# Paged forgetting-attention on one core: preparation two row tiles ahead, prompt part read in place, sample part interleaved

## The chip, the cores and the metric

The kernel runs on one core of one Trainium2 chip. The metric is the device time of one execution in microseconds (us), a median over runs. One execution is one step of a small hybrid decoder (prompt of 1,024 rows, and 8 sample sequences of 8 rows each); the change touches the attention part of its first layer only.

## The reference, cut to what matters

The attention has 8 heads of 64 columns. q and k are normed per head (an RMS norm with a gain), and a log-forget value per row and head, summed along the sequence, is added to the scores.

```python
def fox_attend_prompt(q, k, v, logf):
    Fk = jnp.cumsum(logf, axis=1)
...
    s = einsum('bqhd,bkhd->bhqk', qi, k) * Dh ** -0.5
    s = s + Fq[..., :, None] - Fk[..., None, :]
    s = jnp.where(kpos[None, :] <= qpos[:, None], s, -jnp.inf)
    p = jax.nn.softmax(s, axis=-1)
    return einsum('bhqk,bkhd->bqhd', p, v)

def fox_attend_sample(q, k, v, logf, pool_k, pool_v, pool_lf, page_table):
    k_past = pool_k[page_table]
    v_past = pool_v[page_table]
    lf_past = pool_lf[page_table]
    k_all, v_all = concat(k_past, k), concat(v_past, v)
    Fk = jnp.cumsum(concat(lf_past, logf), axis=1)
...
```

The sample's scores, decay, mask, softmax and values follow as for the prompt; a sequence has 8 pages of 128 past rows. Everything is in 32-bit floats. The output also holds k, v and the log-forgets of the new rows (`fk`, `fv`, `flf`).

## The kernel before, in words

Five engines run their own instruction streams: TensorE (PE, with weight loads shown as PEld), VectorE (DVE), ScalarE (ACT), GpSimd (POOL) and SyncE (SP, which issues most DMAs). The kernel is written with explicit semaphores; each function below is one block, and all engines meet at the end of a block. In the attention three blocks follow one another; what stands on an engine inside one is its program order.

`fox_prep` (L1166) walks over N = 9 row tiles: 8 prompt tiles of 128 rows and one tile of the 64 sample rows. First the log-forgets are made (`fl`, `nab`, `l1`, `lf`), and PE sums them into `psF` by 36 small matmuls (L1281, L1282). Then for each tile: ACT squares the 1,024 columns of q and k (L1265); DVE sums them per head and takes the mean (L1326, L1327) and copies two columns of forget sums into the rows (L1331, L1332); POOL takes the power -1/2 (L1231); DVE scales the rows (L1334); POOL multiplies the gains in (L1235, twice 128x512); PE transposes 16 heads into the one buffer `ps` (L1291); ACT and DVE copy half of it each to `qkA`, two extra rows of which carry the forget sums (L1254, L1318); ACT issues the DMA of `fk` (L1258). ACT closes the block with the sigmoid of the gate `sog` (L1270).

`fox_prompt` (L1341) loads v by one DMA (L1368), which lands in `spare`, the place of the residual `trunk_xT`. In 4 turns of a hardware loop (two heads each) DVE copies q, k and v of a head to staging buffers (L1471 to L1473); then for 16 units PE makes scores and adds the causal mask by a matmul (L1394, L1397), DVE takes the maximum (L1478), ACT the exponential (L1442), PE transposes the probabilities (L1419), ACT copies them (L1453), and PE multiplies with the values (L1406). At a turn's end the outputs are transposed (L1428) and copied (L1456).

`fox_sample` (L1509) handles the 8 sequences one after the other in a hardware loop. SP reads the page table and for each of the 8 pages of a sequence reads one page number and issues three DMAs, log-forgets `lp`, keys `kp` and values `vp` (L1573, L1575, L1577), two sequences ahead of use. The residual saved in `x_kept` (4,352 KB) is brought back by a DMA that ACT issues at the block's start (L1652). Per sequence: DVE spreads the log-forgets (L1695), PE transposes them (L1609), DVE scans them into `F` (L1701); PE turns the keys page by page (L1618), ACT copies them (L1660), PE makes scores of 128 columns (L1623); DVE adds decay and mask into `st` (L1708 to L1710) and takes the maximum (L1711); ACT exponentiates (L1662); PE transposes the probabilities (L1633, L1635), ACT copies them (L1664), PE multiplies with 8 pages of values and the new rows (L1640, L1641); DVE masks the heads (L1715), PE transposes (L1645), DVE sums (L1718). PE holds `pe.wait_ge(reduced, i + 1)` at the end of each sequence, so nothing of the next one starts before.

Of the kernel before, what the change touches and what calls it, by code (L numbers as in the profile page):

```python
# [1165 lines left out]
def fox_prep(nc, C, p, q_gain, k_gain, b_f, qkA, sog, qTs, kTs, lfs, fk, fv, flf):  # L1166
# [6 lines left out]
    N = NT + 1  # L1173
    with Phase(nc, "fxp") as ph:
        pf = ph.sb("pf", [P, 2, 2 * FOX_W])
        gains = ph.sb("gains", [P, 2, DH])
        bf = ph.sb("bf", [P, H])
        sq = ph.sb("sq", [P, 2, 2 * H * DH])
        ss, ms, rstd = (ph.sb(n, [P, 2 * H]) for n in ("ss", "ms", "rstd"))
        fl, nab, l1, lf = (ph.sb(n, [P, N, H]) for n in ("fl", "nab", "l1", "lf"))  # L1180
        qa = ph.sb("qa", [P, 2, 2 * H, A])
        qs = ph.sb("qs", [P, 2 * H, DH])
        ps = ph.ps("ps", [P, 4, 4, P])
        psF = ph.ps("psF", [P, 512])
        F = ph.sb("F", [P, 2, NT, H])
        pf_in = [ph.sem(f"pf_in{b}") for b in range(2)]
        outs = [ph.sem(f"outs{b}") for b in range(2)]
        (params_in, fv_out, sog_in, fl_in, zeroed, nabbed, logged, lf_done, lf_out, summed, squared, meaned,
         rooted, scaled, gained, turned, stored_a, stored_d, dve_step, act_step) = (ph.sem(s) for s in (
             "params_in", "fv_out", "sog_in", "fl_in", "zeroed", "nabbed", "logged", "lf_done", "lf_out", "summed",  # L1190
             "squared", "meaned", "rooted", "scaled", "gained", "turned", "stored_a", "stored_d",
             "dve_step", "act_step"))
# [9 lines left out]
        @block.sync  # L1202
        def _(sp):
            sp.dma_start(gains[:, 0, :], q_gain.partition_broadcast(P)).then_inc(params_in, 16)
            sp.dma_start(gains[:, 1, :], k_gain.partition_broadcast(P)).then_inc(params_in, 16)
            for i in range(N):
                r = rows_of(i)
                if i >= 2:
                    sp.wait_ge(scaled, i - 1)
                sp.dma_start(pf[:r, i % 2, :], p[i * P:i * P + r, 0:2 * FOX_W]).then_inc(pf_in[i % 2], 16)  # L1210
                if i == 1:
                    sp.dma_start(fv, p[:, 2 * FOX_W:3 * FOX_W]).then_inc(fv_out, 16)
                    sp.dma_start(sog[:, 0:NT, :], p[0:SEQ, 3 * FOX_W:4 * FOX_W].rearrange("(n p) c -> p n c", p=P))\
                        .then_inc(sog_in, 16)
                    sp.dma_start(sog[:NS, NT, :], p[SEQ:, 3 * FOX_W:4 * FOX_W]).then_inc(sog_in, 16)
            sp.wait_ge(lf_done, 1)
            sp.dma_start(flf[0:SEQ].rearrange("(n p) c -> p n c", p=P), lf[:, 0:NT, :]).then_inc(lf_out, 16)
            sp.dma_start(flf[SEQ:], lf[:NS, NT, :]).then_inc(lf_out, 16)
            sp.wait_ge(fv_out, 16)
            sp.wait_ge(lf_out, 32)  # L1220

        @block.gpsimd
        def _(pool):
            pool.memset(fl[:], 0.0).then_inc(zeroed, 1)
            pool.wait_ge(params_in, 32)
            pool.tensor_scalar(gains[:, 0, :], gains[:, 0, :], DH ** -0.5, None, ALU.mult).then_inc(params_in, 1)
            pool.wait_ge(params_in, 33)
            for i in range(N):
                r = rows_of(i)
                pool.wait_ge(meaned, i + 1)  # L1230
                pool.tensor_tensor(rstd[:r], ms[:r], C["half"][:r, :2 * H], ALU.pow).then_inc(rooted, 1)  # L1231
                pool.wait_ge(scaled, i + 1)
                for n in range(2):
                    t = rows_out(i)[:, n * H:(n + 1) * H, 0:DH]
                    ins = pool.tensor_tensor(t, t, bc(gains[:r, n, :], 1, H), ALU.mult)  # L1235
                ins.then_inc(gained, 1)

        @block.scalar
        def _(act):
# [5 lines left out]

            act.wait_ge(nabbed, 1)
# [3 lines left out]

            def finish(i):
                act.wait_ge(turned, i + 1)
                if i < NT:
                    ins = act.copy(qkA[:A, 0:8, i * P:(i + 1) * P], ps[:A, 0:2].rearrange("p a b t -> p (a b) t"))  # L1254
                else:
                    ins = act.copy(qTs[:], ps[:, 0, :, :NS])
                ins.then_inc(stored_a, 1)
                act.dma_start(fk[i * P:i * P + rows_of(i), :].rearrange("t (h d) -> t h d", d=DH),  # L1258
                              rows_out(i)[:, H:, 0:DH]).then_inc(outs[i % 2], 16)
            for i in range(N):  # L1260
                r = rows_of(i)
                act.wait_ge(pf_in[i % 2], 16 * (i // 2 + 1))
                if i >= 2:
                    act.wait_ge(meaned, i - 1)
# [6 lines left out]
            act.activation(sog[:NS, NT, :], sog[:NS, NT, :], ACT.Sigmoid)  # L1271
            act.wait_ge(outs[0], 16 * ((N + 1) // 2))
            act.wait_ge(outs[1], 16 * (N // 2))

        @block.tensor
        def _(pe):
            pe.wait_ge(lf_done, 1)
            for i in range(NT):
                o = psF[:, i * H:(i + 1) * H]
                for j in range(i):  # L1280
                    pe.matmul(o, C["ones"][:], lf[:, j, :], start=(j == 0), stop=False)  # L1281
                mm = pe.matmul(o, C["tri"][:], lf[:, i, :], start=(i == 0), stop=True)  # L1282
            mm.then_inc(summed, 1)
            for i in range(N):
                pe.wait_ge(gained, i + 1)
                if i:
                    pe.wait_ge(stored_a, i)
                    pe.wait_ge(stored_d, i)
                if i < NT:
                    for n in range(2 * H):  # L1290
                        mm = pe.transpose(ps[:A, n // 4, n % 4, :], qa[:, i % 2, n, :], C["ident"][:])  # L1291
                else:
                    for n in range(H):
                        mm = pe.transpose(ps[:, n // 4, n % 4, :NS],
                                          qs[:NS, 2 * n:2 * n + 2, :].rearrange("p a d -> p (a d)"),
                                          C["ident"][:NS, :NS])
                mm.then_inc(turned, 1)

        @block.vector
        def _(dve):  # L1300
            step = Chain(dve, dve_step)
            step(dve.memset(qa[:], 1.0))
            dve.wait_ge(fl_in, 48)
            step(dve.tensor_tensor(fl[:], fl[:], bc(bf[:], 1, N), ALU.add))
            dve.scalar_tensor_tensor(nab[:], fl[:], -1.0, fl[:], ALU.mult, ALU.min).then_inc(nabbed, 1)
            dve.wait_ge(logged, 1)
            dve.scalar_tensor_tensor(lf[:], fl[:], 0.0, l1[:], ALU.min, ALU.subtract).then_inc(lf_done, 1)
            dve.wait_ge(lf_done, 1)
            dve.tensor_copy(lfs[:], lf[:NS, NT, :])
# [2834 lines left out]
```

## Time and profile before

| | us |
|---|---|
| median of 3 runs | 4562.07 (4560.52 to 4562.45) |
| the profiled execution's own time | 4567.51 |
| its span, first to last instruction | 4565.8 |
| attention: preparation, prompt, sample | from 971 to 1658 of the span |

### The profile page before, as it was taken

The numbers are of one execution on the slowest core, as the hardware profiler recorded it, in microseconds if no ns is written. First come the engines' busy times: TensorE is split into PE (matmuls) and PEld (weight loads), VectorE is DVE, ScalarE is ACT, GpSimd is POOL, SyncE is SP. The second block draws the span as 40 slices with busy tenths as digits, with TensorE's granted clock in tenths as the row PEclk, the third lists the DMA queues.
The fourth block names the chain that finished last, engine by engine and source line by source line (L and its number), as shares of the span: only waits on it lengthen the run. The fifth ranks groups of instructions, "written<-read, shape, count | busy, mean of one in ns | idle before, by whom it ended". The sixth has DMA issues, their size and how long they took to land. (4 is left out here: it accounts for less than half of the span.)

```text
span 4565.8 us, 65914 instructions
## 1 busy us (share of the span) xinstructions
PE 3912.7 (86%) x24414; PEld 3665.5 (80%) x24414; DVE 2287.5 (50%) x4117; ACT 935.8 (20%) x1738; POOL 1240.7 (27%) x946
## 2 busy tenths in 40 slices
PE   8997688666977778999999789794887779999996
PEld 8996577655754467999999789794787779999996
DVE  3265677433322223655556476414773346655554
ACT  2000332123331111211111122202452021111112
POOL 3222233222000012423323133223443233323321
PEclk9998788756678888999999999996887889999997
DMA  4254111121024311111111022223222221111111
GB/s 171 88 157 156 57 43 25 25 79 49 0 78 129 120 39 40 56 37 51 36 51 46 11 72 90 75 68 79 71 52 66 74 46 51 46 37 51 36 41 48
DMA packets 372258, 290.39 MB, mean 64 GB/s; under 512 B 108647, under 2 KB 333991, under 8 KB 371729
## 3 DMA queue, kind: packets, MB, share of 16 engines
q1 hardware_dynamic: 315656, 228.95, 17.1%
q10 hardware_dynamic: 56460, 59.56, 3.9%
q8 instruction: 87, 1.43, 0.1%
q14 instruction: 55, 0.45, 0.0%
HBM read 216.43 MB, written 73.99 MB: 64 GB/s over the span
## 5 line engine op out<-in xcount | busy, mean ns | idle before, releaser
L983 PE MATMUL fup_acc<-ffn_high,fup_wh 128*128 128x364 f32 (+1 forms) x2112 | 699.5, 331 | 48.6 <-POOL fup_wl L907 26.9
L984 PE MATMUL fup_acc<-ffn_low,fup_wh 128*128 128x364 f32 (+1 forms) x2112 | 698.3, 331 | 0.0
L985 PE MATMUL fup_acc<-ffn_high,fup_wl 128*128 128x364 f32 (+1 forms) x2112 | 696.1, 330 | 0.0
L983 PEld LDWEIGHTS fup_acc<-ffn_high,fup_wh 128*128 128x128 f32 x2112 | 400.4, 190 | 50.6 <-POOL fup_wl L907 25.6
L1143 DVE TENSOR_TENSOR trunk_xT<-fup_dn,trunk_xT 128x364 f32<-128x364 f32 x528 | 282.7, 535 | 245.6 <-PE fup_dn L1001 245.6
L984 PEld LDWEIGHTS fup_acc<-ffn_low,fup_wh 128*128 128x128 f32 x2112 | 400.5, 190 | 0.0
L985 PEld LDWEIGHTS fup_acc<-ffn_high,fup_wl 128*128 128x128 f32 x2112 | 400.3, 190 | 0.0
L999 PE MATMUL fup_dn<-fup_gh,fup_dh 128*128 128x364 f32 (+1 forms) x1056 | 348.4, 330 | 21.3 <-issue 21.3
L1000 PE MATMUL fup_dn<-fup_gl,fup_dh 128*128 128x364 f32 (+1 forms) x1056 | 347.3, 329 | 0.0
L1001 PE MATMUL fup_dn<-fup_gh,fup_dl 128*128 128x364 f32 (+1 forms) x1056 | 346.7, 328 | 0.0
L335 PE MATMUL p_acc<-p_wh,even_in_high 128*128 128x296 f32 (+1 forms) x936 | 281.4, 301 | 10.6 <-DVE even_in_low L374 7.9
L336 PE MATMUL p_acc<-p_wl,even_in_high 128*128 128x296 f32 (+1 forms) x936 | 281.8, 301 | 0.0
L337 PE MATMUL p_acc<-p_wh,even_in_low 128*128 128x296 f32 (+1 forms) x936 | 280.6, 300 | 0.0
L1056 ACT ACTIVATE fup_conv<-fup_hp,fup_cur 128x1024 f32<-128x1024 f32 x88 | 109.6, 1246 | 574.4 <-DVE fup_hs L1118 574.4
L1131 DVE SCALAR_TENSOR_TENSOR fup_conv<-fup_hp,fup_cur,fup_conv 128x1024 f32<-128x1024 f32 x176 | 225.4, 1280 | 3.1
L999 PEld LDWEIGHTS fup_dn<-fup_gh,fup_dh 128*128 128x128 f32 x1056 | 199.3, 189 | 21.8 <-issue 21.8
L907 POOL TENSOR_TENSOR fup_wl<-fup_ws,fup_wh 128x1024 fp32r<-128x1024 f32 x88 | 211.1, 2399 | 7.0
L983 PE MATMUL gqkv_acc<-odd_in_high,gqkv_wh 128*128 128x364 f32 (+1 forms) x576 | 191.4, 332 | 24.2 <-DVE odd_in_low L1086 21.8
L924 POOL COPY fup_cur<-ffn_taps 128x4 f32 (+1 forms) x88 | 16.4, 187 | 711.0 <-DVE fup_conv L1132 711.0
L1115 DVE TENSOR_TENSOR fup_hp<-fup_acc,fup_rs 128x364 f32<-128x364 f32 (+1 forms) x264 | 125.4, 506 | 159.7 <-PE fup_acc L985 145.9
L1000 PEld LDWEIGHTS fup_dn<-fup_gl,fup_dh 128*128 128x128 f32 x1056 | 200.0, 189 | 0.0
L1001 PEld LDWEIGHTS fup_dn<-fup_gh,fup_dl 128*128 128x128 f32 x1056 | 199.1, 189 | 0.0
(719 smaller groups left out, 8674.2 us busy)
## 6 DMA issues: line engine op xcount, KB each, us to landing
fup_ws<-in_ffn_w_up SPq DMA_DIRECT2D x88, 512.0 KB, 4.0
fup_ds<-in_ffn_w_down SPq DMA_DIRECT2D x22, 1024.0 KB, 5.9
fs_kp<-in_cache_fox_k SPq DMA_DIRECT2D x64, 256.0 KB, 2.7
fs_vp<-in_cache_fox_v SPq DMA_DIRECT2D x64, 256.0 KB
ev<-p_o ACTq DMA_DIRECT2D x104, 148.0 KB, 1.8
p_ws<-in_ev_w_in SPq DMA_DIRECT2D x12, 1184.0 KB, 7.1
qkv<-gqkv_conv ACTq DMA_DIRECT2D x24, 544.0 KB
gqkv_ws<-in_od_w_in SPq DMA_DIRECT2D x24, 512.0 KB, 4.1
```

Source lines behind the costliest of these rows:

```text
L335: pe.matmul(ps, xh[:, k, cols], wh[:, b, k], start=(k == 0), stop=False)
L336: pe.matmul(ps, xh[:, k, cols], wl[:, b, k], start=False, stop=False)
L337: mm = pe.matmul(ps, xl[:, k, cols], wh[:, b, k], start=False, stop=(k == KD - 1))
L907: pool.tensor_tensor(wl[:, b], ws[:, b], wh[:, b], ALU.subtract).then_inc(low, 1)
L983: pe.matmul(ps, wh[:, b, k], xh[:, k, c0:c0 + w_], start=(k == 0), stop=False)
L984: pe.matmul(ps, wh[:, b, k], xl[:, k, c0:c0 + w_], start=False, stop=False)
L985: mm = pe.matmul(ps, wl[:, b, k], xh[:, k, c0:c0 + w_], start=False, stop=(k == KD - 1))
L999: pe.matmul(ps, dh[:, s, cols], gh[:, s, c0:c0 + w_], start=(s == 0), stop=False)
L1000: pe.matmul(ps, dh[:, s, cols], gl[:, s, c0:c0 + w_], start=False, stop=False)
L1001: mm = pe.matmul(ps, dl[:, s, cols], gh[:, s, c0:c0 + w_], start=False, stop=(s == 1))
L1131: dve.scalar_tensor_tensor(cp, hp[:, b, j:j + SEQ], cur[:, b, j:j + 1], cp, ALU.mult, ALU.add)
L1143: dve.tensor_tensor(xT[:, t, c0:c0 + w_], dn[m % 2][:, :w_], xT[:, t, c0:c0 + w_], ALU.add).then_inc(added, 1)
```

## The change

Preparation: the tile buffer `pf` has 4 places, and squares and means are issued two tiles ahead of the scaling (AHEAD = 2); `ps` has two buffers; the gains are applied by ACT while it copies both halves from `ps` (a scale per partition, `gcol`), and for `fk` by one DVE multiply (`ko`), which SP stores; the forget sums take 7 adds on DVE (`before`) and two matmuls; SP loads v into `spare` in this block already. Prompt: q, k and v are read where they are, the turns are written out instead of looped, and SP gathers the page table and the 64 pieces of log-forgets of the sample part. Sample: all log-forgets are transposed and scanned once, ahead of the sequences; scores are made 512 columns at a time; decay and mask are added on PE by matmuls (`spread` with `F`, the identity with `causal`); maximum and exponential read PSUM; PE works on the next sequence's keys and scores between one sequence's probabilities, values and `collect`; SP reads a page number for each DMA; the return of `x_kept` is issued by ACT at sequence 1.

```diff
@@ fox_prep, scalar: order of squares and stores
-            for i in range(N):
...
-                act.activation(sq[:r, i % 2], pf[:r, i % 2], ACT.Square).then_inc(squared, 1)
-                if i:
-                    finish(i - 1)
-            finish(NT)
-            act.wait_ge(sog_in, 32)
-            act.activation(sog[:, 0:NT, :], sog[:, 0:NT, :], ACT.Sigmoid)
+            for i in range(AHEAD, N + AHEAD):
+                if i < N:
+                    square(i)
+                if i == N - 1:
+                    act.wait_ge(sog_in, 32)
+                    act.activation(sog[:, 0:NT, :], sog[:, 0:NT, :], ACT.Sigmoid)
+                    act.activation(sog[:NS, NT, :], sog[:NS, NT, :], ACT.Sigmoid)
+                store(i - AHEAD)
@@ fox_prep, vector: one tile
+                if i + AHEAD < N:
+                    mean(i + AHEAD)
...
+                dve.wait_ge(rooted, i + 1)
+                step(dve.tensor_tensor(rows_out(i)[:, :, 0:DH], pf[:r, i % RING, :].rearrange("p (h d) -> p h d", d=DH),
+                                       bc(rstd[:r, i, :], 2, DH), ALU.mult))
+                dve.sem_inc(scaled, 1)
...
+                dve.tensor_tensor(ko[:r, b], rows_out(i)[:, H:, 0:DH], bc(gains[:r], 1, H), ALU.mult).then_inc(ko_done, 1)
@@ fox_sample, sync
+            def load(dst, pool, n, sem):
+                page = sp.value_load(table[0:1, n:n + 1], min_val=0, max_val=N_POOL - 1)
+                sp.dma_start(dst, pool[bass.ds(page, 1)].rearrange("o p c -> p (o c)")).then_inc(sem, 16)
+            for i in seqs:
+                if i >= 2:
+                    sp.wait_ge(k_turned, NU * (i - 1))
+                for g in range(NPG):
+                    load(kp[:, i % 2, g, :], pool_k, i * NPG + g, k_in[i % 2][g // HALF])
+                if i >= 2:
+                    sp.wait_ge(valued, i - 1)
+                for g in range(NPG):
+                    load(vp[:, i % 2, g, :], pool_v, i * NPG + g, v_in[i % 2])
@@ fox_sample, tensor: a key turn and a score of 512 columns
+                for g in range(HALF):
+                    mm = pe.transpose(PS[:, 5 + n % RING, g * P:(g + 1) * P],
+                                      kp[:, i % 2, c * HALF + g, m * P:(m + 1) * P], ident[:])
...
+                pe.matmul(S[:, c * 512:(c + 1) * 512], qx[:, i, m, :], kT[:, n % RING, :], start=(m == 0), stop=False)\
+                    .then_inc(k_used, 1)
```

The order on ACT in the preparation, from the two first squares on (`fxp_sq` is the squares' buffer, `fxp_ps` the turned heads). Before, the store of a tile and its DMA stand ahead of one square:

```order
L1265 ACTIVATE fxp_sq<-fxp_pf 128x1024 x2
L1254 COPY fox_p_qkA<-fxp_ps 66x8x128
L1258 DMA out_fk<-fxp_qa 1024x1x64
L1265 ACTIVATE fxp_sq<-fxp_pf 128x1024
L1254 COPY fox_p_qkA<-fxp_ps 66x8x128
```

And now:

```order
L1266 ACTIVATE fxp_sq<-fxp_pf 128x1024 x2
L1288 ACTIVATE fxp_nab<-fxp_nab 128x72
L1290 ACT_TABLE_LOAD
L1290 ACTIVATE fxp_l<-fxp_nab 128x72
L1266 ACTIVATE fxp_sq<-fxp_pf 128x1024
L1276 ACTIVATE fox_p_qkA<-fxp_ps,fxp_gcol 66x8x128 x2
L1266 ACTIVATE fxp_sq<-fxp_pf 128x1024
L1276 ACTIVATE fox_p_qkA<-fxp_ps,fxp_gcol 66x8x128 x2
```

Three squares (tiles 0, 1 and 2) now stand ahead of the first store, two before; from there on squares and stores still alternate.

The order on DVE in the preparation of the changed kernel, from the first tile of the loop on (`ss` and `ms` are sum and mean, `qa` the scaled rows):

```order
L1327 TENSOR_REDUCE fxp_ss<-fxp_sq 128x16
L1328 TENSOR_SCALAR fxp_ms<-fxp_ss 128x16
L1359 COPY fxp_qa<-fxp_F 128x8
L1360 COPY fxp_qa<-fxp_F 128x8
L1362 TENSOR_TENSOR fxp_qa<-fxp_pf,fxp_rstd 128x16x64
L1367 TENSOR_TENSOR fxp_ko<-fxp_qa,fxp_gains 128x512
```

The first two rows are the sum and mean of tile i + 2, the others belong to tile i; before, all were of one tile.

The order on PE in the sample part of the changed kernel, one stage (L1599 turns keys, L1609 scores, L1628 probabilities, L1638 values, L1645 collects, L1616 to L1620 decay and mask):

```order
L1599 MATMUL fs_PS<-trunk_ident,fs_kp 128x128 x12
L1628 MATMUL fs_PS<-trunk_ident,fs_pr 128x64 x8
L1629 MATMUL fs_PS<-trunk_ident,fs_pr 8x64
L1609 MATMUL fs_PS<-fs_kT,fs_qx 64x512
L1599 MATMUL fs_PS<-trunk_ident,fs_kp 128x128 x4
...
L1638 MATMUL fs_PS<-fs_vp,fs_pT 64x512 x8
L1639 MATMUL fs_PS<-fs_vn,fs_pT 64x512
...
L1645 MATMUL fs_PS<-fs_onehot,fs_om 128x8 x4
L1609 MATMUL fs_PS<-fs_kT,fs_qx 64x512 x3
L1616 MATMUL fs_PS<-fs_F,fs_spread 64x512 x2
```

Twelve key turns of sequence i + 1 stand between the exponential that PE waits for and the probabilities of sequence i; before, nothing of another sequence stood there (L1628 of `fs_N`, then L1633).

## Rows read from the trace of the kernel before

**Rows 1.** Windows: length, busy PE, PEld, DVE, ACT, POOL (instructions), granted clock, DMA share, GB/s.
```profile
971.00:999.20 28.20, 15.53 (x72) 15.44 (x72) 2.72 (x6) 3.70 (x5) 0.56 (x2) 0.50 0.60 203
999.20:1064.10 64.90, 30.10 (x136) 22.47 (x136) 35.05 (x53) 14.76 (x15) 47.07 (x27) 0.50 0.33 86
1080.60:1343.40 262.80, 244.90 (x1216) 196.48 (x1216) 82.12 (x213) 96.22 (x203) 0.00 (x0) 0.73 0.00 0
1343.40:1367.80 24.40, 0.66 (x4) 0.50 (x4) 2.99 (x16) 0.37 (x1) 4.58 (x5) 0.50 0.96 354
1367.80:1657.90 290.10, 225.86 (x1160) 138.59 (x1160) 61.25 (x117) 52.79 (x96) 0.00 (x0) 0.82 0.32 103
1139.80:1180.70 40.90, 39.18 (x134) 30.60 (x134) 11.99 (x29) 13.16 (x29) 0.00 (x0) 0.50 0.00 0
```
**Rows 2.** Timeline, start of the preparation: start, duration, instruction, [idle before].
```profile
983.30 0.23 DVE L1307 SCALAR_TENSOR_TENSOR fxp_lf<-fxp_fl,fxp_l 128x72 f32<-128x72 f32 x1 [1.90 <-ACT fxp_l L1249]
...
999.16 0.22 DVE L1311 COPY fxp_F<-fxp_psF 128x64 f32<-128x64 f32 x1 [15.43 <-PE fxp_psF L1282]
...
1004.08 1.23 DVE L1334 TENSOR_TENSOR fxp_qa<-fxp_pf,fxp_rstd 128x1024 f32<-128x1024 f32 x1 [2.96 <-POOL fxp_rstd L1231]
```
**Rows 3.** Timeline, the steps of one row tile in the preparation.
```profile
1007.75 3.62 PE L1291 MATMUL fxp_ps<-trunk_ident,fxp_qa 128*66 128x128 f32 x16 [8.63 <-POOL fxp_qa L1235]
...
1011.41 1.01 ACT L1254 COPY fox_p_qkA<-fxp_ps 66x1024 f32<-66x1024 f32 x1 [26.25 <-PE fxp_ps L1291]
...
1012.32 1.06 ACT L1265 ACTIVATE fxp_sq<-fxp_pf 128x1024 f32<-128x1024 f32 x1
1013.41 1.22 DVE L1326 TENSOR_REDUCE fxp_ss<-fxp_sq 128x16 f32<-128x1024 f32 x1 [0.46 <-ACT fxp_sq L1265]
...
1014.66 0.17 DVE L1327 TENSOR_SCALAR fxp_ms<-fxp_ss 128x16 f32<-128x16 f32 x1
```
**Rows 4.** Timeline, the scaling of the last tile and the end of the preparation.
```profile
1059.16 1.22 DVE L1334 TENSOR_TENSOR fxp_qs<-fxp_pf,fxp_rstd 64x1024 f32<-64x1024 f32 x1 [3.00 <-POOL fxp_rstd L1231]
...
1065.98 3.62 ACT L1270 ACTIVATE fox_sog<-fox_sog 128x4096 f32<-128x4096 f32 x1
```
**Rows 5.** Timeline, start of the prompt block, and of its second turn.
```profile
1070.36 0.38 SPq L1368 DMA_DIRECT2D trunk_xT<-out_fv  x1
...
1080.61 0.79 PE L1394 MATMUL fx_S<-trunk_xT 66*128 66x128 f32 x2 [16.51 <-DVE fx_vh L1473]
...
1144.19 1.28 ACT L1442 ACT_TABLE_LOAD   x1
1144.35 0.29 DVE L1478 TENSOR_REDUCE fx_mx<-fx_S 128x1 f32<-128x128 f32 x1 [1.97 <-PE fx_S L1397]
```
**Rows 6.** Groups by line, sample part: busy, mean ns, idle before them and releaser.
```profile
L1609 PE MATMUL fs_L<-trunk_ident,fs_lx 128*64 128x128 f32 x64 | 15.0, 416 | 36.5 <-DVE fs_qx L1699 36.5
...
L1633 PE MATMUL fs_psK<-trunk_ident,fs_pr 64*128 64x64 f32 x64 | 8.1, 298 | 34.6 <-ACT fs_pr L1662 34.6
```
**Rows 7.** Timeline, single steps of the first sequence of the sample part.
```profile
1368.70 0.38 SPq L1577 DMA_DIRECT2D fs_vp<-in_cache_fox_v  x1
...
1369.94 0.33 SPq L1573 DMA_DIRECT2D fs_lp<-in_cache_fox_logf  x1
...
1372.91 0.42 PEld L1618 LDWEIGHTS fs_psK<-trunk_ident,fs_kp 128*128 128x128 f32 x4 [0.17 <-issue]
...
1385.57 1.22 DVE L1711 TENSOR_REDUCE fs_mx<-fs_st 64x1 f32<-64x1032 f32 x1
1386.83 1.15 ACT L1662 ACTIVATE fs_pr<-fs_st,fs_mx 64x1032 f32<-64x1032 f32 x1 [4.54 <-DVE fs_mx L1711]
...
1391.56 0.23 PEld L1640 LDWEIGHTS fs_O<-fs_vp,fs_pT 128*64 128x64 f32 x1 [0.62 <-issue]
...
1396.23 0.14 PEld L1640 LDWEIGHTS fs_O<-fs_vp,fs_pT 128*64 128x64 f32 x1 [0.29 <-issue]
```
**Rows 8.** The page's list of DMA issues: count, size of one, us to landing.
```profile
fs_kp<-in_cache_fox_k SPq DMA_DIRECT2D x64, 256.0 KB, 2.7
```

More of the change, by code:

```diff
@@ L1224, in _ @@
             pool.memset(fl[:], 0.0).then_inc(zeroed, 1)
[L1225 to L1227 removed]
+            pool.memset(before[:, 0, :], 0.0).then_inc(zeroed, 1)
+            pool.memset(qa[:], 1.0).then_inc(qa_set, 1)
             for i in range(N):
@@ L1230, in _ @@
                 pool.wait_ge(meaned, i + 1)
[L1231 to L1236, printed above, removed]
+                pool.tensor_tensor(rstd[:r, i, :], ms[:r, i, :], C["half"][:r, :2 * H], ALU.pow).then_inc(rooted, 1)
         @block.scalar
@@ L1276, in _ @@
         def _(pe):
[L1277 to L1283, printed above, removed]
-            for i in range(N):
[L1285 to L1295, printed above, removed]
+            pe.wait_ge(lf_done, 2)
@@ new lines, in _ @@
+            pe.matmul(psF, C["tri"][:], lf[:, 0:NT, :].rearrange("p n h -> p (n h)"), start=True, stop=False)
+            pe.matmul(psF, C["ones"][:], before.rearrange("p n h -> p (n h)"), start=False, stop=True).then_inc(summed, 1)
+            for i in range(N):
+                pe.wait_ge(scaled, i + 1)
+                if i == 1:
+                    pe.wait_ge(F_done, 1)
+                if i >= 2:
+                    pe.wait_ge(stored, i - 1)
+                for n in range(2 * H):
+                    if i < NT:
+                        mm = pe.transpose(ps[i % 2][:A, n // 4, n % 4, :], qa[:, i % 2, n, :], C["ident"][:])
+                    else:
+                        h, k = n % H, n // H
+                        mm = pe.transpose(ps[i % 2][:DH, 2 * k + h % 2, h // 2, :NS], qs[:NS, n, :],
@@ L1430, in body @@
                     mm.then_inc(o_turned, 1)
-            with pe.Fori(0, turns) as i:
+            for i in range(turns):
                 body(i)
@@ L1455, in body @@
                     act.wait_ge(o_turned, i * 2 + (half + 3))
-                    act.copy(mixT[:, bass.ds(i, 1), half * 512:(half + 1) * 512].rearrange("p o t -> p (o t)"),
+                    act.copy(mixT[:, i, half * 512:(half + 1) * 512],
                              psM.rearrange("p a b -> p (a b)")).then_inc(mixed, 1)
             act.sem_inc(copied, 1)
-            with act.Fori(0, turns) as i:
+            for i in range(turns):
                 body(i)
@@ new lines, in _ @@
+            for u in range(8):
+                score(0, u)
+                if u < 5:
+                    turn_keys(0, u + 3)
+            pe.wait_ge(spread_done, 1)
+            pe.wait_ge(masks_done, 1)
+            pe.wait_ge(scanned, 2)
+            pe.wait_ge(gate_copied, 1)
+            decay(0)
+            for i in seqs:
+                nxt = i + 1 < NB
+                if nxt:
+                    for u in range(3):
+                        turn_keys(i + 1, u)
+                turn_probs(i)
+                if nxt:
+                    for u in range(2):
+                        score(i + 1, u)
+                        turn_keys(i + 1, u + 3)
+                values(i)
+                if nxt:
+                    for u in range(2, 5):
+                        score(i + 1, u)
+                        turn_keys(i + 1, u + 3)
+                collect(i)
+                if nxt:
+                    for u in range(5, 8):
+                        score(i + 1, u)
+                    decay(i + 1)
```

507 lines of the change are left out of this document (253 added, 254 removed).

## The prediction, made before the changed kernel ran

> **What bounds the kernel now.** I read the windows first, cut at the blocks of the attention [rows 1]. The preparation (971 to 1070) has no full engine: in its tile loop of 64.9 us PE is busy 30.1, DVE 35.1, ACT 14.8, POOL 47.1, at a granted clock of 0.50. So a chain binds it, not a load. The prompt part is bound by PE: 244.9 of 262.8 us, at a mean clock of 0.73. The sample part begins with 24.4 us of loading (PE busy 0.66, DMA engines 0.96 busy at 354 GB/s), and in the 290.1 us behind it PE is busy 225.9 at a clock of 0.82 while DMA is 0.32 busy. Then I read the groups by line for the sample part, for PE's idle time: 34.6 us stand before the probabilities, released by the exponential, and 36.5 before the transposes of log-forgets, released by DVE's setup of the next sequence [rows 6]. Both are 4.3 to 4.6 us in each of 8 sequences; the reader is to see that a sequence's softmax and its neighbour's setup lie bare on PE, and that in them PE has nothing else to do. The timeline gives the durations of single steps.
>
> The sum is made against the profiled execution (4567.5 us; 5.4 over the median of the runs shown); I take 5.4 off at the end. A measurement of this kernel can tell about 0.2% (9 us) from no change.
>
> **Preparation, the start.** The 36 small matmuls are removed: PE spends 15.5 us on 72 passes [rows 1], and DVE waits 15.43 for them [rows 2]. In their place stand 7 dependent DVE adds and two matmuls. An add costs about the 0.23 us of the neighbouring small operation, so 1.6, and I give the matmuls 0.6. The log-forgets are done at 983.5 [rows 2], so the forget sums are copied by 986.5 rather than 999.5. Behind them DVE does the mean of tile 2 (1.4), the column copies (0.3) and the scaling (1.23): the first tile is scaled at about 990.5 against 1005.3 [rows 2], 15 us earlier.
>
> **Preparation, the loop.** "Two tiles ahead" suggests that squares run free. The order says otherwise. On ACT the square of tile i+2 stands behind the stores of tile i-1, and on DVE the mean of tile i+2 stands ahead of the scaling of tile i. So the scaling of tile i waits for: transposes of i-1, its two stores, square of i+2, mean of i+2, scaling of i. By rows: transposes 3.62 (at the half clock, which the loop has now), two ACT copies 1.01 each with 0.91 from one start to the next, together 1.9, square 1.06 [rows 3], reduce and mean 1.42 from start to end [rows 3], column copies 0.2, scaling 1.23 [rows 2], and some 0.2 of handing over: 9.7 us. Now a tile takes (1059.16 - 1004.08) / 8 = 6.9 [rows 2, 4]. The gains on POOL and one DVE copy are off the path, but a whole chain of three engines is closed in a ring. Six such steps lead from the scaling of tile 0 to that of tile 6: 990.5 + 58 = 1048.7. From there no square is left: tiles 6, 7 and 8 take PE 3.7, 3.7 and about 2.3, and the last stores 1.5; the sigmoid with its table load (1.28 as in the prompt's row, and some 4.2 for both parts [rows 4, 5]) now lies under these transposes. The block ends near 1060 instead of 1070. **Saves 10.** Bounds: if PE's clock rose, transposes take half, a tile 7.9, and it saves 20; if the loads, which now bring v as well before the loop, delay the first tile by 6 us, 4.
>
> By the Trainium skill (TensorE: Matmul & The Clock Gate, section on the array's architectural detail) the queues of ScalarE and VectorE are strictly first in, first out, and only PE may pull weight loads ahead. This trace agrees: the square at 1012.32 follows the copy of 1011.41 at once and did not pass it [rows 3]. If a square could pass a waiting store, tiles would run at PE's pace, which is the second rival below.
>
> **Prompt.** v is loaded in the block before, so the first score comes about 1.1 us after the block's start rather than 1080.61 - 1070.36 = 10.25 [rows 5]: 9.1 saved. The staging copies at a turn's start lie under PE's output transposes and cost nothing now; what cover they had is not needed further. In three turns the table load (1144.19 for 1.28) holds the exponential back by 0.83 behind the maximum, which is done at 1144.64 [rows 5]; with written-out turns I take it as gone, 2.5. The 64 gathers on SP lie beside 262.8 us in which DMA moves nothing [rows 1]. **Saves 11.5**; bounds 8 (the table load stays, the gathers slow one start) to 20 (the half-clock stretch at a turn gets shorter).
>
> **Sample, one stage.** PE's work on a sequence at full clock, from rows: 32 key turns at 0.106 each (0.42 for 4) 3.4 [rows 7]; passes of 512 columns at 0.43 (0.14 and 0.29 [rows 7]): 16 for scores, 4 for decay, 18 for values, 16.3; some 29 small ones at under 0.106, about 2.4. Together 22.1. Idle: maximum 1.22 and exponential 1.15 plus 0.4 of accumulator and handing over, less 1.3 of key turns that now stand there [rows 7], 1.5; and 1.0 for collect and values waiting on copies. A stage is 24.6, and a sequence is 36.3 now (290.1 / 8).
>
> **Sample, loads.** SP reads a page number for each load now. From the issue of vp to the next lp 1.24 us pass, which is one read and one issue [rows 7]. So 17 loads a stage take 20.5, below 24.6 but not far. At the start, the first values wait for the key turns of sequence 1, hence for 21 loads: 21 x 1.24 + 2.7 of landing [rows 8] is 28.7, and with 5 for key turns, probabilities and their copy the values of sequence 0 begin at 33.7.
>
> **Sample, sum.** 33.7 + 6 x 24.6 + 22 (the last stage turns no keys ahead) + 7.7 values + 2.4 tail = 213 at full clock, against 24.4 + 290.1 = 314.5. The clock is the open term. Before the values PE stands idle for 4.3 us, and the values then begin at 0.85 a pass and end at 0.43 [rows 6, 7]; the mean is 0.82. The new bare waits are 1.5 at most, so I expect it higher. If the clock were full, nothing is added; if the mean stayed 0.82, 36% of a stage would lie at half, which makes 24.6 into 30.0, 38 over seven stages. I take a third, 13, nearer the full end since two thirds of the idle time is gone. So 226, **saves 88.5** (63 to 101). The return of `x_kept` (4,352 KB) now falls among page loads: at 354 GB/s [rows 1] it is 12.6 us of DMA, from 0 (hidden by the loads' lead of about a stage) to 12.6. I take 0, as page loads occupy a third of the DMA time now.
>
> By the Trainium skill (DMA: Bandwidth & Descriptors, Issuing engines are not separate DMA queues), DMAs of SP and ACT interleave on the same 16 engines, which speaks against a free return; by it the sample part would be 239. The trace's 0.96 DMA share at the sample's start [rows 1], when both load, agrees.
>
> Together 10 + 11.5 + 88.5 = 110: 4457.5 for a profiled execution, **4452** as a median.
>
> **Rivals.** (a) *The clock stays at half through the whole sample part.* The prompt part shows that PE may be busy 39.18 of 40.90 us with a clock of 0.50 throughout [rows 1], so being busy alone does not bring it up; against it, the sample part has 0.82 with more gaps. A stage then has 44.2 of PE's work and 2 idle, 46.2, and the sample part 379: 64.5 more than before, 4562 - 21.5 + 64.5 = **4605**. It decides from a stage of 42 us on (336 less 44 for start and end, over 7), that is with 80% of the stage at half clock. (b) *The preparation really runs two ahead*: a tile is PE's 3.7, the block ends at about 1028, 32 more saved: **4420**. The order speaks against it. (c) *SP binds the sample part*: if each load cost the whole 2.2 of today's set of three, a stage is 17 x 2.2 = 37 and nothing is saved there: about **4545**. Three issues in a set with one read speak against it. (d) *Full clock in every stage*: **4439**. (e) *Clock as low as now, 0.82*: 25 more, **4477**.
>
> **Numbers.** Forecast with its neighbourhood (4443 to 4468) 0.59; (a) 0.05; (b) 0.06; (c) 0.05; (d) 0.12; (e), with the return of `x_kept` exposed, 0.13. The range reaches from (b) past (e) with the return: 4418 to 4490; it leaves out (a) and (c), one in ten. Faster by over 0.2%: all but (a) and the 0.02 between the signs, 0.93; the same 0.02; slower 0.05.
>
> **What would show it.** The start: the copy of forget sums at about 986. The loop: 9.7 us from one scaling to the next, each square right behind a store, and DVE idle before the mean, released by ACT's square; wrong if 3.7 or 6.9. The prompt: first score a microsecond after the block begins, no table load at a turn. The sample: stages of 25 to 28 us, idle before the probabilities near 1.5 each, key loads never the releaser but at the start, a clock over 0.9. What would make the prediction wrong above all is the clock in the sample part, then the start of its loads.

## The result, and the profile after

The changed kernel takes 4436.33 us (median of 4 runs, 4427.01 to 4457.23) against 4562.26 before: a ratio of 0.973, with a 95% interval of 0.969 to 0.976. That is 126 us faster; 4452 was predicted. The profiled executions differ by 4567.51 - 4435.05 = 132.5 us. Every median below is taken over the fast runs, which leaves out one run of e10 that took 11393 us.

I cut both traces at the same four instructions: the memset of `fl` on POOL (preparation), that of the mask (prompt), the copy of the turned gate `sgT` on ACT (sample), and the first cast of the output projection behind them (end).

| block, us | before | after | won | predicted |
|---|---|---|---|---|
| preparation | 97.7 | 83.7 | 14.0 | 10 |
| prompt | 274.0 | 243.1 | 30.9 | 11.5 |
| sample | 313.4 | 231.1 | 82.3 | 88.5 |
| outside the attention | | | 5.3 | 0 |

The windows of the changed kernel (columns as in [rows 1]), first its blocks, then five stretches of the prompt part:

```profile
969.50:985.50 16.00, 1.12 (x4) 0.93 (x4) 6.78 (x24) 4.87 (x6) 7.76 (x5) 0.50 0.81 289
985.50:1053.60 68.10, 28.04 (x144) 21.70 (x144) 25.82 (x46) 29.63 (x29) 27.66 (x7) 0.62 0.39 128
1054.70:1297.10 242.40, 225.53 (x1220) 182.10 (x1220) 71.14 (x192) 92.69 (x201) 0.50 (x1) 0.80 0.02 2
1297.10:1321.00 23.90, 18.30 (x74) 9.04 (x74) 7.07 (x16) 5.05 (x9) 4.17 (x5) 0.79 0.72 220
1321.00:1528.20 207.20, 188.51 (x728) 76.95 (x728) 17.35 (x25) 45.68 (x89) 0.00 (x0) 0.97 0.50 160
1092.60:1119.20 26.60, 24.09 (x167) 20.07 (x166) 9.24 (x26) 10.53 (x22) 0.00 (x0) 1.00 0.07 5
1119.80:1146.80 27.00, 26.32 (x88) 20.24 (x87) 6.32 (x16) 8.64 (x22) 0.00 (x0) 0.50 0.02 2
1147.20:1180.80 33.60, 30.60 (x213) 25.47 (x211) 11.18 (x31) 14.00 (x29) 0.00 (x0) 1.00 0.00 1
1181.40:1208.00 26.60, 25.92 (x86) 19.82 (x86) 6.32 (x16) 7.63 (x20) 0.00 (x0) 0.50 0.00 0
1208.60:1294.00 85.40, 77.25 (x524) 63.49 (x523) 29.25 (x80) 38.12 (x82) 0.00 (x0) 1.00 0.00 1
```

The reader is to see two things. PE worked during the first loading of the sample part (18.3 of 23.9 us, where it had 0.66 of 24.4 [rows 1]). And the prompt part still is PE's, but at a clock of 0.80 instead of 0.73. Both begin with a stretch at half (35 us before, 38 after). Behind the ends of the first two turns the clock now lay at half for 27 us each, where one such stretch before was 40.9 [rows 1], and from 1208.6 to 1294.0, across the third turn's end, it stayed at full.

One tile of the preparation, in the timeline of the changed kernel (start, duration, instruction, [idle before]):

```profile
994.80 1.22 DVE L1362 TENSOR_TENSOR fxp_qa<-fxp_pf,fxp_rstd 128x1024 f32<-128x1024 f32 x1
...
996.13 3.62 PE L1313 MATMUL fxp_ps<-trunk_ident,fxp_qa 128*66 128x128 f32 x16 [5.94 <-DVEq L1364]
...
999.79 2.11 ACT L1276 ACTIVATE fox_p_qkA<-fxp_ps,fxp_gcol 66x1024 f32<-66x1024 f32 x2 [6.51 <-PE fxp_ps L1313]
1001.80 1.05 ACT L1266 ACTIVATE fxp_sq<-fxp_pf 128x1024 f32<-128x1024 f32 x1
1002.88 1.22 DVE L1327 TENSOR_REDUCE fxp_ss<-fxp_sq 128x16 f32<-128x1024 f32 x1 [6.02 <-ACT fxp_sq L1266]
...
1004.36 1.22 DVE L1362 TENSOR_TENSOR fxp_qa<-fxp_pf,fxp_rstd 128x1024 f32<-128x1024 f32 x1
```

This is the ring of the prediction: it goes from DVE to PE, to ACT and back to DVE, each starts when the one above it ends, and from one scaling to the next it is 9.56 us (9.7 worked out, 6.9 before [rows 2, 4]). Each of the three engines is idle for about 6 of them.

### The profile page after: what moved, and what is told of

Same layout as the page of the kernel before. It is cut to its first block and busy times, and to the rows that moved or that the text cites. A ratio compares the mean times of both kernels' runs of the same rounds, so it can differ in the third digit from the quotient of the medians.

```text
span 4433.3 us, 64635 instructions
## 1 busy us (share of the span) xinstructions
PE 3850.3 (87%) x23996; PEld 3574.0 (81%) x23996; DVE 2240.9 (51%) x4008; ACT 939.4 (21%) x1746; POOL 1227.3 (28%) x929
## 5 line engine op out<-in xcount | busy, mean ns | idle before, releaser
L999 PEld LDWEIGHTS fup_dn<-fup_gh,fup_dh 128*128 128x128 f32 x1056 | 199.3, 189 | 21.8 <-issue 21.8
L983 PE MATMUL gqkv_acc<-odd_in_high,gqkv_wh 128*128 128x364 f32 (+1 forms) x576 | 191.3, 332 | 27.5 <-DVE odd_in_low L1086 25.0
```

The costliest lines, as they stand in the source:

```text
L983: pe.matmul(ps, wh[:, b, k], xh[:, k, c0:c0 + w_], start=(k == 0), stop=False)
L999: pe.matmul(ps, dh[:, s, cols], gh[:, s, c0:c0 + w_], start=(s == 0), stop=False)
```

## The experiments

Each kernel was timed beside the kernel before, and the ratio is to that. Blocks and "clock", the granted clock of the prompt block, are those of one profiled execution each.

| kernel | preparation | prompt (clock) | sample | median | ratio to before |
|---|---|---|---|---|---|
| before | 97.7 | 274.0 (0.73) | 313.4 | 4562.26 | |
| changed | 83.7 | 243.1 (0.80) | 231.1 | 4436.33 | 0.973 (0.969 to 0.976) |
| e1 preparation alone | 84.2 | 269.5 (0.76) | 310.3 | 4547.05 | 0.996 (0.995 to 0.997) |
| e2 prompt alone | 97.7 | 252.4 (0.80) | 310.2 | 4536.39 | 0.994 (0.992 to 0.997) |
| e3 sample alone | 97.6 | 278.3 (0.72) | 233.3 | 4488.88 | 0.984 (0.981 to 0.986) |
| e4 mean behind | 57.9 | 230.1 (0.86) | 235.2 | 4405.41 | 0.967 (0.964 to 0.969) |
| e5 turns written out | 97.8 | 232.3 (0.88) | 310.1 | 4535.18 | 0.994 (0.992 to 0.996) |
| e6 paired units | 57.7 | 252.6 (0.78) | 235.9 | 4444.09 | 0.975 (0.971 to 0.979) |
| e7 return at start | 60.6 | 230.1 (0.86) | 244.0 | 4414.04 | 0.967 (0.963 to 0.971) |
| e8 pairs grouped | 57.2 | 230.2 (0.86) | 233.7 | 4407.43 | 0.966 (0.963 to 0.970) |
| e9 turns joined | 57.3 | 213.7 (0.91) | 231.1 | 4396.27 | 0.962 (0.958 to 0.965) |
| e10 stall at turns | 57.6 | 267.3 (0.74) | 235.6 | 4445.67 | 0.972 (0.970 to 0.974) |
| e11 changed again | 89.9 | 223.3 (0.88) | 237.3 | 4434.14 (one run) | |
| e12 turns joined, again | 57.9 | 213.7 (0.91) | 231.7 | 4392.89 | 0.963 (0.962 to 0.965) |

### One part alone: e1, e2, e3

e1 puts the changed `fox_prep`, without its load of v, into the kernel before; e2 the changed `fox_prompt`, with v loaded at its start and without the gathers; e3 the changed `fox_sample`, with the gathers on SP in the old prompt block:

```diff
 e2, fox_prompt, sync
-            for n in range(NB * NPG):
-                page = sp.value_load(table[0:1, n:n + 1], min_val=0, max_val=N_POOL - 1)
...
+            sp.dma_start(v[:], fv[0:SEQ, :].rearrange("(t p) c -> p t c", p=P)).then_inc(v_in, 16)
```

> The changed preparation (without its early load of v) in the kernel before; prompt and sample as before. Theory: the new order closes a ring of 9.6 us a tile, so only the 15 us at the start and the hidden sigmoid are won against 6.9 us a tile: the block is 14 us shorter (98.1 to about 84), the whole 0.3% faster (4548). Rival: some of the 14 us comes with the early load or with the clock of the neighbouring blocks; then the block is shorter by less than 10.

> The changed prompt part (read in place, turns written out) in the kernel before; v is still loaded at the block's start, nothing is gathered. Theory: the 30.5 us that the block lost are 9.1 of waiting for v and some 21 of clock, and the clock is won by the written-out turns, which leave fewer gaps at a turn's start: this kernel's block is 18 to 24 us shorter than 273. Rival A: the clock has nothing to do with the code, only with when the block starts, so the shares of half clock may come out as before or anywhere: 0 to 24. Rival B: only the table loads go: 2.5 shorter, half-clock stretches as before.

> The changed sample part in the kernel before, with the gathers of log-forgets and of the page table on SP in the old prompt block. Theory: parts add up, the sample block takes 232 us instead of 314.6 with stages of 27 us; the whole 82 us faster (4480). Rival: the sample part gains from the clock with which the new prompt block hands over (full at its end there, half in the kernel before): then the start is slower and the block takes 240 or more.

The preparation block is 13.5 us shorter, the prompt block 21.6, the sample block 80.1. The parts add up within the intervals: by the ratios 18.7 + 26 + 73.5, with 9.1 for the early v, 127 of 124 to 126. The sample part doesn't need the new prompt block ahead of it. e2 shows that 21.6 us of the prompt part have nothing to do with the wait for v.

Of the sample part's gain the windows show what kind of time went. PE's idle time in the block fell from 88 us (314.5, less 0.66 and 225.86 busy [rows 1]) to 24 (231.1, less 18.30 and 188.51), and its busy time from 227 to 207. So about three quarters are idle time that is now filled. How much each edit gives (the early scan, scores of 512 columns, decay on PE, the next sequence's keys in the gaps) no run takes apart.

### The ring of the preparation: e4

```diff
             for i in range(N):
                 r, b = rows_of(i), i % 2
-                if i + AHEAD < N:
-                    mean(i + AHEAD)
...
                 dve.tensor_tensor(ko[:r, b], rows_out(i)[:, H:, 0:DH], bc(gains[:r], 1, H), ALU.mult).then_inc(ko_done, 1)
+                if i + AHEAD < N:
+                    mean(i + AHEAD)
```

> The changed kernel with one thing moved in the preparation: DVE does the mean of tile i + 2 behind the scaling of tile i, not ahead of it. Theory of the ring: the scaling no longer waits for the square that stands behind the last tile's store; a round of the chain now spans three tiles, (9.6 + 3 of POOL) / 3 = 4.2 us a tile, near PE's 3.7; the block is some 30 us shorter (84 to about 54), the whole near 4405. Rival: the tile time is set by something else (the loads of pf, the stores, PE at half clock), and the tiles stay above 8 us: 4430.

The block falls from 83.7 to 57.9 us, and the median by 31. Two rows of its timeline show what became of the wait:

```profile
1008.30 1.22 DVE L1327 TENSOR_REDUCE fxp_ss<-fxp_sq 128x16 f32<-128x1024 f32 x1 [1.87 <-ACT fxp_sq L1266]
...
1013.80 1.23 DVE L1360 TENSOR_TENSOR fxp_qa<-fxp_pf,fxp_rstd 128x1024 f32<-128x1024 f32 x1 [0.48 <-POOL fxp_rstd L1251]
```

DVE waited about 6 us for each square of the ring (6.02 above); now it waits 1.87 here, 2.57 at one other tile, and not at all at the rest, and a scaling waits at most 0.79 for POOL's power. The scalings of tiles 0 and 7 start 34.5 us apart, 4.9 a tile; 4.2 was expected. The ring is shown: nothing but the place of one pair of instructions differs. (Of the median's 31 us the preparation explains 26; the profiles' prompt blocks differ as well, for which see e11.)

### What the prompt part gained: e5, e6

e5 keeps the staging copies and the wait for v, and only writes the turns out, on PE, ACT and DVE:

```diff
-            with pe.Fori(0, turns) as i:
+            for i in range(turns):
                 body(i)
```

> The kernel before with its prompt part's four turns written out instead of looped; the staging copies and the wait for v stay. It tells apart what the prompt part owes to the written-out turns and to reading in place. Theory A: the loop's costs at a turn (table load, branch) let the clock fall longer: the block drops from 274 to about 254, as with the whole changed prompt part. Theory B: it is the staging, which holds the scores of a head until three copies are through: the block stays at 268 or more. Rival: neither, only where in time the block lies; then its share of half clock differs from both with no relation to the edit.

The block takes 232.3 us, 41.7 less than before, where 254 was expected, at a clock of 0.88. The profile is of the fastest of 8 runs; by the medians e5 is 31.5 us faster than the kernel before, and e2 29. Either way the written-out turns alone are enough for the prompt part's gain beyond the wait for v, and nothing has to be put down to reading in place. In the three profiles with the loop (before, e1, e3) the block took 269.5 to 278.3 us, and written out, with the wait for v of 9.1, 232.3 and 252.4 (e5, e2). The windows of e5: the block, the stretch at half behind the first turn, and the one after it:

```profile
1071.50:1302.80 231.30, 202.11 (x1220) 165.01 (x1220) 83.22 (x216) 92.45 (x202) 0.87 (x1) 0.88 0.03 11
1139.60:1145.60 6.00, 4.88 (x20) 4.11 (x20) 2.33 (x6) 1.63 (x4) 0.00 (x0) 0.50 0.01 3
1146.60:1237.60 91.00, 83.12 (x551) 67.45 (x551) 37.86 (x99) 42.78 (x92) 0.00 (x0) 1.00 0.00 1
```

Up to 1139 e5 and the kernel before do the same at the same moment, and the clock falls in both at the first turn's end. Before it stayed at half for 40.9 us [rows 1], here for 6 or 7, and after it the next turn's end didn't lower it; the third's did, for 14 us. The loop's table load doesn't begin the fall: before, the clock was at half from 1139.8, and the load came at 1144.19 [rows 5]. The runs show that with the loop the clock stays at half for longer, not which of the loop's costs does it.

e6 is e4 with another order of a turn's 16 units:

```diff
+        unit = [(u % 2, u // 2 if u % 2 == 0 else NT - 1 - u // 2) for u in range(U)]
...
-                hb, qt = divmod(u, NT)
+                hb, qt = unit[u]
```

> The kernel with the mean behind the scaling, and in the prompt part the 16 units of a turn in another order: a short row tile of one head beside a long one of the other (0 and 7, 1 and 6, and so on), so that PE's work for a unit no longer shrinks to one tile at a turn's start. Theory: the clock falls where the units are short and PE waits for the softmax between them; with even units the half-clock share (0.28 of the block there) falls and the block takes 195 to 215 instead of 230, the whole 4385. Rival: the clock falls at a turn's end for the output transposes and their copies; the order of the units changes nothing, 230.

A miss: 252.6, 22 us longer than e4's, with a fall at each turn's end. Even units don't keep the clock up. PE waits more often: for ACT's copy of the probabilities 20 times in the block, 13.8 us in all, against 12 times and 9.9 us in e4. At the first turn's end, where a short unit now stands last, it waits 0.68, 0.80, 0.54, 0.45 and 0.68 us. That these waits are the reason is not shown.

### The turn's end itself: e9, e10, e11, e12

e9 is e8 (below) with the turns joined: the 64 units run as one sequence on PE, ACT and DVE, and a turn's output transposes stand behind the next turn's first unit.

```diff
-            for i in range(turns):
-                body(i)
+            score(0, 0)
+            for g in range(turns * U):
+                i, u = divmod(g, U)
+                if g + 1 < turns * U:
+                    score(*divmod(g + 1, U))
...
+                if g:
+                    value(*divmod(g - 1, U))
+                if g and not u:
+                    outputs(i - 1)
```

e10 is e4 with a small stall instead:

```diff
             def body(i):
+                if i:
+                    act.activation(idle[:], mask[:, 0:1], ACT.Sigmoid)
                 exp(i, 0)
```

> The kernel with the mean behind the scaling and the pairs grouped, and the prompt part's turns joined: the next turn's first two scores and its first probabilities stand ahead of a turn's last values and output transposes on PE, and so on ACT and DVE. Theory: TensorE's clock falls at a turn's end, where PE waits some 0.5 and 0.7 us for DVE and ACT and then has the shortest units; without these waits it falls less often, and the block takes 200 to 222 instead of 230. Rival: it falls for the short units alone, which stay; then 226 to 230 (a few us for the waits themselves).

> The kernel with the mean behind the scaling, and in the prompt part one sigmoid of a single column on ACT at the start of turns 1 to 3, so that the exponential's table must be loaded again as in the loop of the kernel before; it holds the first exponential of a turn some 2 us back. The output is the same. Theory: such a stall at a turn's start is what the loop cost; beyond its own 6 us the clock falls at each turn and stays at half for some 40 us as in the kernel before: the block takes 250 to 265 instead of 230. Rival: the clock doesn't mind a short stall of the exponential, since PE has scores to make: 230 to 238.

> The changed kernel once more, for a second look at where the clock falls in its prompt part. Theory: the stretches follow from the code, so they lie at the turns again, the last turn undisturbed, block 243. Rival: they are chance of the moment: another number of falls, a block that differs by 10 or more.

e10's block takes 267.3 us, 37 more than e4's, though the three stalls themselves leave PE idle for 6.5 (1.81, 1.81 and 2.85); by the medians it is 40 us slower. e9's block takes 213.7, 16 less than e8's. The windows of e10, its block and the stretches behind its first three turns:

```profile
1037.80:1304.10 266.30, 245.02 (x1220) 196.33 (x1220) 71.14 (x192) 101.04 (x210) 0.51 (x1) 0.74 0.02 2
1101.60:1138.60 37.00, 34.51 (x112) 26.05 (x113) 7.90 (x19) 12.99 (x27) 0.00 (x0) 0.50 0.02 1
1170.60:1196.60 26.00, 24.18 (x79) 18.17 (x77) 6.33 (x16) 9.62 (x22) 0.00 (x0) 0.50 0.00 0
1238.60:1268.60 30.00, 30.00 (x98) 22.67 (x97) 7.19 (x17) 8.59 (x18) 0.00 (x0) 0.50 0.00 1
```

And of e9, its block, the stretch at half at its start, and what follows up to the last turn's end:

```profile
1030.60:1243.30 212.70, 197.79 (x1220) 161.79 (x1220) 71.13 (x192) 92.17 (x202) 0.51 (x1) 0.91 0.03 2
1031.00:1055.50 24.50, 24.50 (x81) 18.79 (x81) 6.33 (x16) 7.42 (x20) 0.00 (x0) 0.50 0.07 5
1056.50:1229.50 173.00, 160.71 (x1086) 131.97 (x1085) 63.88 (x172) 81.83 (x177) 0.00 (x0) 1.00 0.02 2
```

Two readings need care. First, e10's stall is larger than what it stands for: before, the table load left PE idle for 0.40 us at a turn. And at the ends of e10's first two turns the clock had fallen (by 1101.6 and 1169.8) before the stall came (PE waited 1.81 us until 1108.46 and until 1174.84). So e10 shows that a stall there lengthens the block by far more than itself; how it does so stays open.

Second, joining the turns does not take all of PE's waits away. The first turn's end in e8, and then in e9:

```profile
1079.04 1.06 PE L1445 MATMUL fx_psT<-trunk_ident,fx_pr 128*128 128x128 f32 x8 [1.39 <-ACT fx_pT L1479]
...
1082.15 1.97 PE L1432 MATMUL fx_psO<-trunk_xT,fx_pT 128*128 128x64 f32 x16 [0.54 <-DVE fx_o L1515]
1084.57 1.12 PE L1454 MATMUL fx_psM<-trunk_ident,fx_o 128*128 128x128 f32 x4 [0.45 <-DVE fx_o L1515]
1086.36 1.12 PE L1454 MATMUL fx_psM<-trunk_ident,fx_o 128*128 128x128 f32 x4 [0.68 <-ACT even_mix_foxT L1482]
```

```profile
1084.49 1.06 PE L1453 MATMUL fx_psT<-trunk_ident,fx_pr 128*128 128x128 f32 x8 [0.89 <-ACT fx_pT L1487]
...
1090.06 0.66 PE L1441 MATMUL fx_psM<-trunk_ident,fx_o 128*128 128x128 f32 x4 [0.45 <-DVE fx_o L1510]
1091.39 0.66 PE L1441 MATMUL fx_psM<-trunk_ident,fx_o 128*128 128x128 f32 x4 [0.68 <-ACT even_mix_foxT L1476]
```

The waits of 0.45 and 0.68, the 0.5 and 0.7 of the expectation, are still there. What went is the 0.54, and 1.39 became 0.89: 3.06 us of waiting became 2.02. With that, no inner turn's end lowers the clock. The last turn's end is not joined, and there all four waits stand as in e8, and the clock fell.

e11 warns against reading one profile: the changed kernel a second time had a prompt block of 223.3 and the clock fell only near the ends of the third and the fourth turn, not at the first two as in the first profile, with its 243.1. So where the waits at a turn's end stay, a fall is a matter of the moment; in each of these kernels it came at a turn's end or up to some 10 us around it. That is why e9 was run once more:

> The kernel with the turns joined once more, since one look can't tell its clock from chance (the changed kernel's own prompt block came out at 243 and 223). Theory: without the waits at a turn's end the clock stays up over the inner turns each time: the block again below 222, the median below 4400. Rival: the first look was luck; the block is at 223 to 243, the median at 4405 or above.

The block took 213.7 again with the same stretches, and the median of 5 runs is 4392.89 (4382.62 to 4397.15). This version beats both kernels: 168 us, 3.7%, less than the kernel before timed beside it. Against e8, without the joining, the medians are 11 (e9) and 15 us (e12) lower, but the intervals of the ratios overlap; the block, 16.5 us shorter in both profiles, tells more.

Counted over all profiles, the clock fell at 9 of 9 inner turns' ends with the loop (before, e1, e3), at 10 of 21 with written-out turns (changed, e2, e4, e5, e7, e8, e11), at 6 of 6 in e6 and e10, and at 0 of 6 with the turns joined (e9, e12). Behind these ends it lay at half for 99 to 123 us of a block with the loop and for 14 to 65 with written-out turns.

### The sample part's terms: e7, e8

e7 is e4 with ACT's `act.dma_start(back[0], back[1])` moved from sequence 1 to the block's first place:

> The kernel with the mean behind the scaling, and the return of the saved residual (4352 KB) issued at the sample block's start again, not at sequence 1. Theory: at the start it stands beside the first key pages, which PE waits for: the sample part's start is up to 12.6 us later (4352 KB at 354 GB/s), so the block takes 240 to 248 instead of 235, the whole 4410 to 4418. Rival: the queues share and the first keys come nearly as early: within 3 us, 4405.

The block is 8.8 us longer. The first key turn of e7 shows the wait, which in e4 is not there:

```profile
1278.47 2.82 PE L1599 MATMUL fs_PS<-trunk_ident,fs_kp 128*128 128x128 f32 x12 [9.39 <-DMA fs_kp<-in_cache_fox_k]
```

So issuing the return later is worth about 9 us, and where it stands now it costs nothing: of the page loads only one key load (0.81 us, at the first key turn of sequence 1) ever holds PE in the changed kernel. The medians, 4414 and 4405, are too near to tell by themselves.

e8 is e4 with two scores and then two key turns:

```diff
-                    for u in range(2):
-                        score(i + 1, u)
-                        turn_keys(i + 1, u + 3)
+                    score(i + 1, 0)
+                    score(i + 1, 1)
+                    turn_keys(i + 1, 3)
+                    turn_keys(i + 1, 4)
```

> The kernel with the mean behind the scaling, and in the sample part two scores, then two key turns, instead of one and one. A stage came out at 27.3 us where 24.6 was worked out; in it a pair of a score and a key turn takes 1.59 where the durations sum to 1.28. Theory: each change between scores and key turns costs PE 0.15, so four changes less a stage bring 0.6 us a stage, 26.7, 5 us in all. Rival: the pair waits for ACT's copy of the keys (0.59 each); then grouped ones wait longer and the stage takes 27.3 or more.

In the trace a full-clock stage takes 25.92 us (from the maximum at 1333.63 to that at 1359.55) against 26.49 in e4 (1308.71 to 1335.20): 0.57 less, as worked out from the changes of form. But the expected 5 us in all didn't come. The mean of e8's seven stages is 27.32 (from 1278.48 to 1469.75), as in the changed kernel, where 26.7 was expected: a stage in which the clock falls once takes some 27.5 in e8, and six of its seven stages are such, against three of seven in the changed kernel (28.08 each). e9 and e12, with the same grouping, have 27.21 and 27.34. So the grouping won its time on PE and the clock took it back; the medians (4407 and 4405) show no gain either.

## Why the prediction was right, point by point

**The start of the preparation.** Right: the forget sums are copied at 983.39 in a block that began 2.7 us earlier, so at 986.1 on the old scale (986.5), and the adds took 1.39 (1.6).

**The ring.** Right: 9.56 us (9.7), and e4 shows the cause. The block won 4 us more than predicted, since transposes ran in part at full clock in the last tiles (5.63 us for two of 3.62) and the first scaling came 2.3 us sooner than worked out. The size of it changes with the execution: in e11 the same kernel's block took 89.9, 2 less won than predicted. Its ring was the same (9.56), but its first scaling came 5 us later in the block, as DVE waited 5.16 us for the load of `fl` where it had waited 0.33. By the Trainium skill (TensorE: Matmul & The Clock Gate, section on the array's architectural detail) ScalarE's queue is first in, first out; the trace agrees, as no square passed a store in any tile.

**The wait for v.** Right: PE starts 1.11 us after the block's first DMA in the changed kernel, 10.25 before [rows 5], and it waits for the mask, not for v.

```profile
1053.62 0.27 SPq L1392 DMA_DIRECT2D fox_table<-in_page_table  x1
...
1054.73 0.77 PE L1422 MATMUL fx_S<-fox_p_qkA 66*128 66x128 f32 x2 [3.98 <-POOL fx_mask L1404]
```

**The table load.** This is the step that failed, by a factor of eight: "In three turns the table load ... holds the exponential back by 0.83 behind the maximum ...; with written-out turns I take it as gone, 2.5". It is gone (the changed kernel's second turn has its maximum at 1122.85 and its exponential at 1123.17, without one). But I priced the stall by its own length, and left the clock of the prompt part as it was but for a bound "to 20". The block won 30.9, beyond that bound: 9.1 for v, and 21.8 for the clock and the stalls. The clock's part follows from the windows: half-clock shares of 0.54 of 263 us and 0.40 of 242 are 142 and 97 us, and 45 us less at half are worth about 22. e5 puts this on the written-out turns. That a stall at a turn's start can cost as much is shown by e10, with stalls longer than the loop's, and that shorter waits at its end spare the inner falls by e9 and e12. Which of the loop's costs it was stays open. In e11 the block won 51 where the first profile won 31, so the size of this term changes with the execution.

**The stage of the sample part.** 24.6 was predicted, 27.3 came (the first maximum at 1320.95, the eighth at 1511.97). The idle time fits in sum only: 2.10 us before the probabilities, where 1.5 was worked out, and next to none of the 1.0 for collect and values. PE's work was too small: a score (0.86) and a key turn (0.42) follow each other every 1.59 us, not 1.28, as these weight loads show (a score's two passes stand as x2, a key turn's four transposes as x4):

```profile
1406.11 0.57 PEld L1628 LDWEIGHTS fs_PS<-trunk_ident,fs_pr 64*128 64x128 f32 x8 [2.10 <-ACT fs_pr L1711]
...
1406.80 0.19 PEld L1609 LDWEIGHTS fs_PS<-fs_kT,fs_qx 128*64 128x64 f32 x2
1407.80 0.43 PEld L1599 LDWEIGHTS fs_PS<-trunk_ident,fs_kp 128*128 128x128 f32 x4 [0.81 <-issue]
1408.39 0.19 PEld L1609 LDWEIGHTS fs_PS<-fs_kT,fs_qx 128*64 128x64 f32 x2 [0.16 <-issue]
```

Each change between the two forms costs 0.14 to 0.17. Five pairs make 1.5 us of a stage, and e8 shows it on a stage at full clock, where four changes less gave 0.57. The same loss stood in the rows of the kernel before (0.17 ahead of a key turn [rows 7]), where I took only the durations of single instructions.

**The clock in the sample part.** Right in direction: 0.95 over the block, short falls once a stage or less. 13 us were taken for it; 231 - 213 = 18, less 7 x 1.9 for the stage at full clock (26.5, not 24.6), leaves some 5. The stages agree: three of the seven have one short fall, 1.6 us each.

**The loads and the return.** Right: hidden but for 0.8 us. By the Trainium skill (DMA: Bandwidth & Descriptors, Issuing engines are not separate DMA queues) ACT's and SP's DMAs interleave on the same engines; e7 agrees, with 9.4 us of waiting for 12.6 us of bytes. It decides nothing where the loads run a stage ahead.

**The rivals and the total.** None of the rivals came. By its number (d), 4439, is the nearest, and 4436 lies below the forecast's own neighbourhood of 4443 to 4468; but (d) says full clock in every stage, and three of seven had a fall. What brought the total there is the prompt part, 19 us over its term, with 4 over in the preparation, 5 outside the attention that no term covers, and the sample part 6 under its own. That it stayed in the range is owed to the width that the sample part's clock asked for; for the prompt part it is luck. (b) would have been e4's kernel: 4405, where 4420 was named.

## What to carry to other kernels

"Two tiles ahead" is a claim on the order of each queue: follow one tile through every engine's program order, and where a step waits for an instruction that stands behind the last tile's last step, the chain is a ring, whatever the loop is called. A stall of a microsecond or two in a PE-bound loop may cost far more than its length if the clock stays low behind it: look at the granted clock behind a similar gap in the trace, in more than one execution, and put the next turn's work into a loop's end. Take the cost of a group of matmuls from the distance between two groups of the same kind in a row of the trace, not from the sum of single durations, and judge a gain there by the mean of all stages, since the clock can take it back.

## What of the hardware was not expected

Stalls at three turns, 6.5 us of PE's idle time in all, made a block of PE's work 37 us longer (e4 230.1, e10 267.3). The clock lay at half for 26 to 37 us behind each turn, in which PE was busy 88.7 of 93 us; behind the third, in 30.0 of 30.0. The same changed kernel had two patterns of clock in two executions, 20 us apart in one block (243.1 and 223.3). What decides the moment of a fall stays open. PE's waits at a turn's end seem to bear on it: in e9 and e12, where they were cut from 3.06 to 2.02 us, the clock fell at none of six inner ends, and it fell at both last ends, where they stand uncut. That the waits alone decide is not shown, since about half of the written-out turns kept the clock up with all of them in place.
